# Up and gated projections with stationary weights and [high|low] activations as one moving operand

## Chip, cores and metric

One core of one Trainium2 chip. The metric is the device time of one execution in microseconds, the median of several runs. All arithmetic is float32; the matrix products are made exact enough by splitting each operand into a high part (rounded to float32r, "fp32r" in the rows) and a low part (what is left), with three products: high x high, high x low, low x high.

## What is computed

Two transformer blocks on 256 tokens of width 1024. Cut to what the change touches:

```python
# first block
h2 = rmsnorm(x, g_norm2) * (1.0 + scale2) + shift2
x = x + gate2 * (jnp.square(jax.nn.relu(h2 @ w_mlp1)) @ w_mlp2)      # 1024 -> 4096 -> 1024

# second block: four times (two layers, two each)
def swiglu(x, w_gu, w_down):                                           # 1024 -> 2 x 2816 -> 1024
    g, u = jnp.split(x @ w_gu, 2, axis=-1)
    return (jax.nn.silu(g) * u) @ w_down
x = layer_norm(DEEPNORM_ALPHA * x + 0.5 * swiglu(x, w_gu[i, j], w_down[i, j]), ln_g, ln_b)
```

Around these stand two attentions with their projections and a pooling mixer, which the change leaves alone.

## The kernel before

**Weight units.** All large weights come as units of 2 MB, listed by `weight_units` (L72). A wide unit is 1024 input rows by 512 output columns (8 k-tiles of 128 x 512); a deep unit is 512 rows by 1024 columns. The units of this case are `("up", 0..7)`, each with 512 hidden features, and `("gu", f, 0..10)` for the four gated layers f (f0 to f3 below), each with 256 columns of g and 256 of u, then the `down` and `dn` units behind them. A gated layer runs gu 0 to 6, dn 0 to 3, gu 7 to 10, dn 4 and 5. `up` runs 0 to 3, down 0 to 3, up 4 to 7, down 4 to 7.

**Each unit is used for two blocks**, token half 0 and token half 1. `PAIRS` (L124) names units which go with their neighbour as (u,0), (u+1,0), (u,1), (u+1,1): up 0 and 1, gu 0 and 1, down 6 and 7, dn 4 and 5 are such pairs. All others go (u,0), (u,1).

**Four engines, each with one hand-written order.** SyncE loads a unit in two halves into RAW (`raw_load`, L563), a half when the half before it is split. ScalarE rounds four quarters into WH (`round_unit`, L1176, row line L1187), VectorE subtracts into WL (`split_unit`, L1555, row line L1564). WH and WL hold two units. TensorE multiplies. Each engine works its list strictly in order and waits on semaphores.

**A wide block (L738)** is 8 k-tiles of the helper `three` (L724): three matmuls of 512 moving columns, the weights moving (WH, WL, WH), the activations of 128 tokens stationary (AH, AH, AL). The result, tokens by 512 features, stands in one PSUM bank: UP has two banks, used in turn. `up_phase` on ScalarE (L1416) applies Relu or Silu to it (row line L1429), on VectorE (L1905) a product gives TMP (L1920). The deep products want features on the partitions, so TensorE turns TMP with transposes into a TB bank (`from_tmp`, L799, row line L796; four 128x128 blocks for `up`, two for `gu`), always after the block that follows. ScalarE rounds the turned tile to HH (`high`, L1190, row line L1193), VectorE writes HL (`low`, L1567, row line L1570) and so frees the TB bank, of which there are two.

**In `up_phase` of ScalarE and VectorE** the next unit's rounding and splitting stand ahead of a unit's first block; then the block's own activation and product; then the `late` tile, the one turned since. After the last wide block `down_phase` (L1440, L1932) first rounds and splits the unit behind the first deep one, then handles the late tile.

**Deep blocks (L758, `down_phase` L1035)** read HH and HL of one token half; before each block `ready` waits until `need[i]` of that token half is there.

Of the kernel before, what the change touches and what calls it, by code (L numbers as in the profile page):

```python
# [26 lines left out]
P = 128  # L27
TOK = 2
# [117 lines left out]

def wide_keys(first, end):

    return [UNITS[u][0] + (tok,) for u, tok in WIDES if first <= u < end]


def psum_turns():
# [36 lines left out]
    return {k: i for i, k in enumerate(keys)}  # L189


TURN = psum_turns()
# [4 lines left out]
def counts(chosen):  # L197

    n, out = 0, {}
    for k in TURN:  # L200
        if chosen(k):
            n += 1
            out[k] = n
    return out


SPLIT_NO = counts(lambda k: k[0] not in PLAIN)
TMP_S = counts(lambda k: k[0] in BY_SCALAR)
TMP_V = counts(lambda k: k[0] not in BY_SCALAR and k[0] not in ("col", "h", "tab", "ada", "F", "pool", "y", "my"))
TG_NO = counts(lambda k: k[0] in ("up", "gu"))  # L210
TG_AT = {n: TMP_V[k] for k, n in TG_NO.items()}


def key_kt(key):

    return 4 * (key[1] % 4) if key[0] == "up" else 2 * (key[2] % CUT)

# [16 lines left out]
def build(nc, t, out):  # L234
    with ExitStack() as ctx:
# [13 lines left out]
        AH = sb("AH", [P, KT, 256], F32R)  # L249
        AL = sb("AL", [P, KT, 256], F32R)  # L250
# [79 lines left out]
        UP = [bank(f"UP{i}") for i in range(TOK)]  # L330
        Y = [[bank(f"Y{i}{h}") for h in range(2)] for i in range(TOK)]
        TB = [bank(f"TB{i}") for i in range(2)]
# [23 lines left out]
        tg_done = sem("tg_done")  # L356
        s_done = sem("s_done")
# [61 lines left out]
        up_emptied = []  # L419
        copies = 0  # L420
        for u, tok in WIDES:
            name = UNITS[u][0]
            k = name[0]
            if k == "misc":
                up_emptied.append((lf_in, tok + 1))
            elif k in ("vd", "vf", "gate") or (k == "moba" and name[1] >= 4):
                copies += 1
                up_emptied.append((up_copied, copies))
            elif k in BY_SCALAR:
                up_emptied.append((tmp_s, TMP_S[name + (tok,)]))  # L430
            elif k == "up":
                up_emptied.append((tg_done, TG_NO[name + (tok,)]))
            else:
                up_emptied.append((tmp_v, TMP_V[name + (tok,)]))

        def up_bank(u, tok):

            return Y[1][tok] if u == 1 else UP[WIDE_NO[u, tok] % 2]

# [283 lines left out]
        def _(pe):  # L723
# [14 lines left out]
            def wide(u, tok, chain=None, turns=None, head=None):  # L738

                _, _, width, kts = UNITS[u]  # L740
                pe.wait_ge(*up_emptied[WIDE_NO[u, tok] - (4 if u == 2 else 2)])
                ts = slice(tok * P, (tok + 1) * P)
                dst = up_bank(u, tok)
                for k in range(kts):
# [10 lines left out]
                    quarter_taken(mm, u, tok, (k + 1) * width)  # L755
                mm.then_inc(mm_done, 1)
# [25 lines left out]
            def bank_of(key):  # L782
                b = TURN[key]
                if b >= 2:
                    pe.wait_ge(*emptied(b - 2))
                return TB[b % 2]
# [236 lines left out]
            def up_phase(units, blocks, chain, buf, late):  # L1023

                first = UNIT[units[0]]
                for u, tok in [blk for blk in WIDES if first <= blk[0] < first + len(units)]:
                    opening = chain and u < first + 2
                    wide(u, tok, chain if opening else None,
                         (chain, 1, buf) if opening and (u, tok) == (first + 1, 0) else None)
                    for k in late:  # L1030
                        from_tmp(k, blocks)
                    late = [UNITS[u][0] + (tok,)]
# [135 lines left out]
        def _(act):  # L1168
# [21 lines left out]
            def high(key, dst, n):  # L1190
# [3 lines left out]
                         ).then_inc(th_done, 1)  # L1194

# [219 lines left out]

            def up_phase(units, nblk, func, chain, late):  # L1416
                first = UNIT[units[0]]
                n = P * nblk
                for u, tok in [blk for blk in WIDES if first <= blk[0] < first + len(units)]:
# [6 lines left out]
                    act.wait_ge(mm_done, MM_NO[u, tok])  # L1426
                    if TG_NO[key] > 2:
                        act.wait_ge(tmp_v, TG_AT[TG_NO[key] - 2])
                    act.activation(tg_of(key)[:, 0:n], up_bank(u, tok)[:, 0:n], func).then_inc(tg_done, 1)  # L1429
# [7 lines left out]
                    late = [(key, HH[:, k0:k0 + nblk, tok * P:(tok + 1) * P])]  # L1437
                return late

            def down_phase(units, late, n, last=False):  # L1440
                for i, unit in enumerate(units):
                    if not (last and i == len(units) - 1):
                        round_unit(UNIT[unit] + 1)
                    if i == 0:
                        for k, dst in late:
                            high(k, dst, n)
# [100 lines left out]
        def _(ve):  # L1547
# [356 lines left out]

            def up_phase(units, nblk, square, chain, late):  # L1905
                first = UNIT[units[0]]
                n = P * nblk
                for u, tok in [blk for blk in WIDES if first <= blk[0] < first + len(units)]:
# [6 lines left out]
                    b = TURN[key]  # L1915
                    ve.wait_ge(tg_done, TG_NO[key])
                    ve.wait_ge(tr_done, b - 1)
                    tg = tg_of(key)[:, 0:n]
                    other = tg if square else up_bank(u, tok)[:, n:2 * n]
                    ve.tensor_tensor(TMP[:, b % 2, 0:n], tg, other, ALU.mult).then_inc(tmp_v, 1)  # L1920
                    if opening and (u, tok) == (first, 0):
                        chain_low(chain, 1)
                    for k, hi, lo in late:
                        low(k, lo, hi, n)
                    if opening and (u, tok) == (first, 1):
                        split_unit(u + 2, (2, 3))
                    k0 = key_kt(key)
                    at = (slice(None), slice(k0, k0 + nblk), slice(tok * P, (tok + 1) * P))
                    late = [(key, HH[at], HL[at])]
                return late  # L1930

            def down_phase(units, late, n, pieces=0, last=False):  # L1932
                for i, unit in enumerate(units):
                    if not (last and i == len(units) - 1):
                        split_unit(UNIT[unit] + 1)
                    if i == 0:
                        for k, hi, lo in late:
                            low(k, lo, hi, n)
# [153 lines left out]
```

## Time and profile before

| | us |
|---|---|
| median of 3 runs | 1363.24 (1362.72 to 1363.39) |
| span of the profiled execution, first to last instruction | 1361.6 |
| TensorE busy in it | 1333.7 |
| VectorE busy | 824.2 |
| ScalarE busy | 653.3 |
| mean granted TensorE clock | 0.996 of 2.4 GHz |

The median is 1.6 us above the span; I carry that difference unchanged. In rows of a timeline the first number is the start in us from the span's start, the second the duration in us, then engine, line, operation, output<-inputs, shape and count; a bracket at the end gives the idle time just before and what ended it. A matmul's duration includes its way through the array, so the pace of a stream is read from starts, not from durations. An "x4" row is four instructions merged, its duration that of the four.

### The profile page before, as it was taken

Reading aid. Unit: us, or ns where it says so; the run is one execution under the profiler, and the core shown is the slowest. Engines: PE = TensorE matmul, PEld = TensorE weight load, DVE = VectorE, ACT = ScalarE, POOL = GpSimd, SP = SyncE. Lnnn points to the kernel's source line nnn. Section 1 sums busy time; section 2 is a strip of 40 time slices with the busy share of each in tenths; the row PEclk is TensorE's granted clock in tenths of the full one; section 3 lists DMA queues with packets and bytes.
Section 4 is the critical chain, followed back from the end, with each engine's and each line's share of the span. In section 5 each row is a group of like instructions: output and inputs, shape, how many; then the busy total and the mean of one; then the engine's idle time right before and its main releaser. Section 6 shows DMA issues by size and latency. Waiting matters only on the chain.

```text
span 1361.6 us, 16419 instructions
## 1 busy us (share of the span) xinstructions
PE 1333.7 (98%) x6285; PEld 1100.4 (81%) x6285; DVE 824.2 (61%) x1132; ACT 653.3 (48%) x1046; POOL 80.2 (6%) x114
## 2 busy tenths in 40 slices
PE   7999999999999999999999999999999999999997
PEld 6788878888888888888877888888888888888885
DVE  6787667866566554555547554566554566755454
ACT  4675564553454444444665443445443444544342
POOL 1401100100002000001001000001000010100000
PEclk9999999999999999999999999999999999999998
DMA  9957745557555754647516655647645565665551
GB/s 341 320 199 240 268 160 185 185 213 251 185 186 169 231 187 155 206 165 241 192 63 201 201 186 189 211 156 234 201 168 186 186 211 189 208 194 186 190 181 61
DMA packets 160217, 268.38 MB, mean 197 GB/s; under 512 B 9755, under 2 KB 103052, under 8 KB 160012
## 3 DMA queue, kind: packets, MB, share of 16 engines
q1 hardware_dynamic: 152492, 239.49, 51.8%
q0 software_dynamic: 7648, 27.85, 5.7%
q8 instruction: 50, 0.82, 0.2%
q14 instruction: 27, 0.22, 0.1%
HBM read 266.21 MB, written 1.07 MB: 196 GB/s over the span
## 4 chain that ended last, share of the span: by engine, by line
PE 93%; DVE 3%; DMA 1%; issue 1%; ACT 1%; POOL 1%; SPq 0%; DVEq 0%; ACTq 0%; POOLq 0%
PE UP L725 18%; PE UP L727 18%; PE UP L726 18%; PE Y L725 10%; PE Y L727 10%; PE Y L726 10%; PE TB L796 4%; PE Y L828 1%; PE Y L835 1%; DMA WADA<-in_w_ada 0%; DMA ADA<-in_b_ada 0%; DVE ADA L1685 0%; DVE WL L1564 0%; PE TB L871 0%; PE Y L827 0%
## 5 line engine op out<-in xcount | busy, mean ns | idle before, releaser
L1564 DVE TENSOR_TENSOR WL<-RAW,WH 128x1024 fp32r<-128x1024 f32 (+2 forms) x438 | 503.1, 1194 | 185.6 <-ACT WH L1187 180.1
L1187 ACT CAST WH<-RAW 128x1024 fp32r<-128x1024 f32 (+2 forms) x438 | 425.8, 1032 | 219.1 <-PE Y L727 115.7
L725 PE MATMUL UP<-WH,AH 128*128 128x512 f32 (+1 forms) x1120 | 452.4, 404 | 2.9 <-DVE AL L1720 1.3
L727 PE MATMUL UP<-WH,AL 128*128 128x512 f32 (+1 forms) x1120 | 437.4, 391 | 0.0
L726 PE MATMUL UP<-WL,AH 128*128 128x512 f32 (+1 forms) x1120 | 435.9, 389 | 0.0
L725 PEld LDWEIGHTS UP<-WH,AH 128*128 128x128 f32 x1120 | 211.0, 188 | 45.5 <-issue 2.8
L727 PEld LDWEIGHTS UP<-WH,AL 128*128 128x128 f32 x1120 | 210.7, 188 | 45.5
L726 PEld LDWEIGHTS UP<-WL,AH 128*128 128x128 f32 x1120 | 211.5, 189 | 39.9 <-issue 0.2
L725 PE MATMUL Y<-WH,HH 128*128 128x512 f32 (+1 forms) x496 | 193.9, 391 | 0.0
L727 PE MATMUL Y<-WH,HL 128*128 128x512 f32 (+1 forms) x496 | 191.6, 386 | 0.0
L726 PE MATMUL Y<-WL,HH 128*128 128x512 f32 (+1 forms) x496 | 191.4, 386 | 0.0
L1429 ACT ACTIVATE TG<-UP 128x256 f32<-128x256 f32 (+1 forms) x104 | 43.3, 416 | 280.1 <-PE UP L727 280.0
L1920 DVE TENSOR_TENSOR TMP<-TG,UP 128x256 f32<-128x256 f32 x88 | 36.8, 418 | 176.9 <-ACT TG L1429 176.6
L727 PEld LDWEIGHTS Y<-WH,HL 128*128 128x128 f32 x496 | 93.1, 188 | 19.1
L726 PEld LDWEIGHTS Y<-WL,HH 128*128 128x128 f32 x496 | 93.3, 188 | 18.1
L725 PEld LDWEIGHTS Y<-WH,HH 128*128 128x128 f32 x496 | 93.2, 188 | 18.0
L647 POOL TENSOR_SCALAR VAR<-SQ 128x1 f32<-128x1 f32 x18 | 16.8, 935 | 1014.6 <-ACT PR L1205 1011.3
L725 PE MATMUL Y<-WH,AH 128*128 128x512 f32 x144 | 58.0, 403 | 1.0 <-DVE AL L1570 1.0
L727 PE MATMUL Y<-WH,AL 128*128 128x512 f32 x144 | 56.2, 391 | 0.0
L726 PE MATMUL Y<-WL,AH 128*128 128x512 f32 x144 | 56.1, 390 | 0.0
L1193 ACT CAST HH<-TB 128x256 fp32r<-128x256 f32 (+1 forms) x108 | 43.9, 407 | 17.8 <-PE TB L796 14.9
L1570 DVE TENSOR_TENSOR HL<-TB,HH 128x256 fp32r<-128x256 f32 (+1 forms) x108 | 50.5, 468 | 2.7 <-ACT HH L1193 2.2
(236 smaller groups left out, 920.1 us busy)
## 6 DMA issues: line engine op xcount, KB each, us to landing
RAW<-in_ffn_w_gu SPq DMA_DIRECT2D x176, 512.0 KB, 4.9
RAW<-in_ffn_w_down SPq DMA_DIRECT2D x80, 512.0 KB, 4.1
RAW<-in_w_mlp SPq DMA_DIRECT2D x64, 512.0 KB, 4.3
RAW<-in_w_in SPq DMA_DIRECT2D x34, 512.0 KB, 5.5
PIECE<-in_w_ada POOLq DMA_DIRECT2D x32, 512.0 KB, 6.1
RAW<-in_a_w_in SPq DMA_DIRECT2D x24, 512.0 KB, 4.6
WADA<-in_w_ada SPq DMA_DIRECT2D x14, 512.0 KB, 10.1
RAW<-in_w_out SPq DMA_DIRECT2D x8, 512.0 KB, 3.9
```

The source lines that it names most:

```text
L647: step(gp.tensor_scalar(VAR[:, tok:tok + 1], a, b, eps, ALU.add, ALU.add))
L725: pe.matmul(dst, ah, wh, start=first, stop=False)
L726: pe.matmul(dst, ah, wl, start=False, stop=False)
L727: return pe.matmul(dst, al, wh, start=False, stop=last)
L796: mm = pe.transpose(dst[:, i * P:(i + 1) * P], source[:, i * P:(i + 1) * P], order[:, :])
L828: pe.matmul(dst[:, P:REV], q[:, P:256], k[:, 0:256], start=kind == "m", stop=True).then_inc(s_done, 1)
L1187: act.copy(WH[:, u % 2, q * n:(q + 1) * n], raw_half(u, q // 2)[:, (q % 2) * n:(q % 2 + 1) * n]).then_inc(wh_done, 1)
L1193: act.copy(dst, TB[TURN[key] % 2][:, 0:n].rearrange("p (k n) -> p k n", n=dst.shape[2])).then_inc(th_done, 1)
L1429: act.activation(tg_of(key)[:, 0:n], up_bank(u, tok)[:, 0:n], func).then_inc(tg_done, 1)
L1564: ve.tensor_tensor(WL[:, u % 2, o], raw_half(u, q // 2)[:, (q % 2) * n:(q % 2 + 1) * n], WH[:, u % 2, o].bitcast(F32), ALU.subtract).then_ ...
L1570: ve.tensor_tensor(dst, TB[TURN[key] % 2][:, 0:n].rearrange("p (k n) -> p k n", n=dst.shape[2]), hi.bitcast(F32), ALU.subtract).then_inc(t ...
L1920: ve.tensor_tensor(TMP[:, b % 2, 0:n], tg, other, ALU.mult).then_inc(tmp_v, 1)
```

## The change

All `up` and `gu` units except the pairs (up 0, 1 and gu f 0, 1) are computed "by feature": 6 up units and 9 x 4 = 36 gu units. For these, a 128 x 128 piece of the weights is stationary, and the activations move: AH and AL now lie side by side as `AHL`, 512 columns = [256 tokens high | 256 tokens low]. One matmul of WH against all 512 columns and one of WL against the 256 high columns replace the three; the bank then holds high products in columns 0 to 255 and, in 256 to 511, the two corrections. A unit still has two parts, but a part is two 128-feature blocks (for gu: one of g, one of u) for all 256 tokens, in two PSUM banks at once. Even parts use both UP banks (`UPP`), odd parts both TB banks (`TBB`). The result already has features on partitions, so nothing is turned. ScalarE copies the correction columns to TMP, VectorE adds them to the others into TG, then the activation and product follow from SBUF, the rounding to HH and the subtraction to HL from TMP. Numbers of turns (`TURN`) count only what is still turned, and a bank's previous user is looked up in tables.

```diff
+def by_feature(key):
+
+    return key[0] in ("up", "gu") and key[:-1] not in PAIRS and (key[0],) + key[1:-2] + (key[-2] - 1,) not in PAIRS
...
+def turn_banks_before():
+
+    last, out = [None, None], {}
+    for k in ORDER:
+        if not by_feature(k):
+            out[k] = last[TURN[k] % 2]
+            last[TURN[k] % 2] = k
+        elif FEATURE_NO[k] % 2:
+            out[k] = tuple(last)
+            last = [k, k]
+    return out
...
+def feature_kts(key):
+
+    n = 2 if key[0] == "up" else 1
+    k0 = key_kt(key) + n * key[-1]
+    return slice(k0, k0 + n)
...
+        AHL = sb("AHL", [P, KT, 512], F32R)
+        AH, AL = AHL[:, :, 0:256], AHL[:, :, 256:512]
...
+        def turn_bank_free(key):
+
+            return (fs_done, FEATURE_NO[key] + 1) if by_feature(key) else emptied(TURN[key])
+
+        def hidden_ready(key):
+
+            return (fl_done, FEATURE_NO[key] + 1) if by_feature(key) else emptied(TURN[key])
...
+            def feature(u, part, inner=None):
+
+                _, _, width, kts = UNITS[u]
+                key = UNITS[u][0] + (part,)
+                banks = feature_banks(key)
+                order = [(k, block) for k in range(kts) for block in range(2)]
+                if inner is not None:
+                    order.sort(key=lambda kb: kb[1])
+                for k, block in order:
+                    if k == 0:
+                        if block and inner is not None:
+                            from_tmp(*inner)
+                        if FEATURE_NO[key] % 2:
+                            pe.wait_ge(*turn_bank_free(TURNED_BEFORE[key][block]))
+                        else:
+                            pe.wait_ge(*up_emptied[up_before[u, part][block]])
+                    quarters(u, part, (k + 1) * width)
+                    col = k * width + (2 * P * block + P * part if key[0] == "gu" else P * (2 * part + block))
+                    w = slice(col, col + P)
+                    pe.matmul(banks[:, block, :], WH[:, u % 2, w], AHL[:, k, :], start=k == 0, stop=False)
+                    mm = pe.matmul(banks[:, block, 256:512], WL[:, u % 2, w], AH[:, k, :], start=False,
+                                   stop=k == kts - 1)
+                    if block:
+                        quarter_taken(mm, u, part, (k + 1) * width)
+                mm.then_inc(mm_done, 1)
...
@@ up_phase, TensorE
+                    key = UNITS[u][0] + (tok,)
+                    if by_feature(key):
+                        feature(u, tok, (late[0], blocks) if late else None)
+                        late = []
+                        continue
@@ down_phase, TensorE
-                    ready(need[i] + (tok,))
+                    key = need[i] + (tok,)
+                    if by_feature(key):
+                        key = need[i] + (1,)
+                    pe.wait_ge(*hidden_ready(key))
@@ up_phase, ScalarE (behind round_unit(u + 1), as before)
+                        f = FEATURE_NO[key]
+                        act.wait_ge(mm_done, MM_NO[u, tok])
+                        act.wait_ge(tr_done, turned[f % 2])
+                        if f >= 2:
+                            act.wait_ge(fl_done, f - 1)
+                        act.copy(feature_tmp(key).rearrange("p (b n) -> p b n", b=2),
+                                 feature_banks(key)[:, :, 256:512]).then_inc(fc_done, 1)
+                        for k, dst in late:
+                            hidden_high(k, dst, n)
+                        late = []
+                    if by_feature(key) and key[0] == "gu":
+                        act.wait_ge(fs_done, FEATURE_NO[key] + 1)
+                        act.activation(tg_of(key)[:, 0:n], tg_of(key)[:, 0:n], func).then_inc(tg_done, 1)
@@ up_phase, VectorE (behind split_unit(u + 1), as before)
+                        ve.wait_ge(fc_done, FEATURE_NO[key] + 1)
+                        ve.tensor_tensor(tg.rearrange("p (b n) -> p b n", b=2), banks[:, :, 0:256],
+                                         tmp.rearrange("p (b n) -> p b n", b=2), ALU.add).then_inc(fs_done, 1)
+                        for k, hi, lo in late:
+                            hidden_low(k, lo, hi, n)
+                        if square:
+                            ve.wait_ge(fs_done, FEATURE_NO[key] + 1)
+                            ve.scalar_tensor_tensor(tmp, tg, 0.0, tg, ALU.max, ALU.mult).then_inc(tmp_v, 1)
+                        else:
+                            ve.wait_ge(tg_done, LIT_NO[key])
+                            ve.tensor_tensor(tmp[:, 0:n], tg[:, 0:n], tg[:, n:2 * n], ALU.mult).then_inc(tmp_v, 1)
@@ down_phase, ScalarE and VectorE
-                            high(k, dst, n)
+                            hidden_high(k, dst, n)
...
-                            low(k, lo, hi, n)
+                            hidden_low(k, lo, hi, n)
```

`hidden_high` and `hidden_low` do as `high` and `low` did, for a by-feature part from TMP instead of a TB bank; the last of them signals `fl_done`.

## Rows read from the trace of the kernel before

**Rows 1.** The page: busy time by engine, and the chain's shares by engine.
```profile
PE 1333.7 (98%) x6285; PEld 1100.4 (81%) x6285; DVE 824.2 (61%) x1132; ACT 653.3 (48%) x1046; POOL 80.2 (6%) x114
...
PE 93%; DVE 3%; DMA 1%; issue 1%; ACT 1%; POOL 1%; SPq 0%; DVEq 0%; ACTq 0%; POOLq 0%
```

**Rows 2.** Timeline of PE, 1126 to 1133: 512-column matmuls, then twelve of 256 columns.
```profile
1126.88 0.39 PE L725 MATMUL Y<-WH,AH 128*128 128x512 f32 x1
...
1131.41 0.39 PE L727 MATMUL Y<-WH,AL 128*128 128x512 f32 x1
1131.63 0.28 PE L725 MATMUL Y<-WH,HH 128*128 128x256 f32 x1
...
1132.95 0.28 PE L727 MATMUL Y<-WH,HL 128*128 128x256 f32 x1
```

**Rows 3.** Timeline of PE: transposes between blocks, of up (first two) and of gu.
```profile
268.42 0.60 PE L796 MATMUL TB<-IDENT,TMP 128*128 128x128 f32 x4
274.35 0.60 PE L796 MATMUL TB<-IDENT,TMP 128*128 128x128 f32 x4
...
862.56 0.38 PE L796 MATMUL TB<-IDENT,TMP 128*128 128x128 f32 x2
868.25 0.38 PE L796 MATMUL TB<-IDENT,TMP 128*128 128x128 f32 x2
```

**Rows 4.** Timeline of PE, ACT, DVE, 760 to 764: layer f1, end of block (gu 2, 0).
```profile
761.86 0.38 PE L796 MATMUL TB<-IDENT,TMP 128*128 128x128 f32 x2
...
760.55 2.00 ACT L1187 CAST WH<-RAW 128x1024 fp32r<-128x1024 f32 x2 [1.65 <-DMA RAW<-in_ffn_w_gu]
762.46 0.37 ACT L1429 ACTIVATE TG<-UP 128x256 f32<-128x256 f32 x1
...
763.91 0.41 DVE L1920 TENSOR_TENSOR TMP<-TG,UP 128x256 f32<-128x256 f32 x1
```

**Rows 5.** The same place in f0, f2, f3 (PE, DVE) and in up 2 (DVE).
```profile
459.05 0.38 PE L796 MATMUL TB<-IDENT,TMP 128*128 128x128 f32 x2
...
948.77 0.38 PE L796 MATMUL TB<-IDENT,TMP 128*128 128x128 f32 x2
...
1194.63 0.38 PE L796 MATMUL TB<-IDENT,TMP 128*128 128x128 f32 x2
...
462.85 0.41 DVE L1920 TENSOR_TENSOR TMP<-TG,UP 128x256 f32<-128x256 f32 x1
...
951.45 0.41 DVE L1920 TENSOR_TENSOR TMP<-TG,UP 128x256 f32<-128x256 f32 x1
...
1196.60 0.41 DVE L1920 TENSOR_TENSOR TMP<-TG,UP 128x256 f32<-128x256 f32 x1
...
275.58 0.69 DVE L1920 TENSOR_TENSOR TMP<-TG 128x512 f32<-128x512 f32 x1
```

**Rows 6.** Timeline of ACT, up 2: rounding of a turned tile of 512 columns.
```profile
275.04 0.58 ACT L1193 CAST HH<-TB 128x512 fp32r<-128x512 f32 x1
```

**Rows 7.** Timeline of PE, ACT, DVE, 896 to 904: f1, end of (gu 10, 1).
```profile
896.72 0.38 PE L796 MATMUL TB<-IDENT,TMP 128*128 128x128 f32 x2
...
896.92 0.39 ACT L1429 ACTIVATE TG<-UP 128x256 f32<-128x256 f32 x1 [5.05 <-PE UP L727]
...
897.45 3.90 ACT L1187 CAST WH<-RAW 128x1024 fp32r<-128x1024 f32 x4
...
898.55 4.63 DVE L1564 TENSOR_TENSOR WL<-RAW,WH 128x1024 fp32r<-128x1024 f32 x4 [0.45 <-ACT WH L1187]
903.24 0.42 DVE L1570 TENSOR_TENSOR HL<-TB,HH 128x256 fp32r<-128x256 f32 x1
```

**Rows 8.** Windows around a fall of the clock: busy by engine, PEclk, DMA share, GB/s.
```profile
20.00:23.50 3.50, 2.68 (x21) 2.38 (x19) 2.85 (x8) 1.09 (x2) 0.00 (x0) 0.98 1.05 385
23.50:26.50 3.00, 2.94 (x11) 2.94 (x12) 2.79 (x10) 2.13 (x4) 0.00 (x0) 0.50 1.06 388
26.50:30.00 3.50, 3.50 (x22) 3.19 (x22) 3.43 (x4) 0.85 (x1) 0.00 (x0) 0.96 1.05 387
```

More of the change, by code:

```diff
@@ L204, in counts @@
     return out
-SPLIT_NO = counts(lambda k: k[0] not in PLAIN)
+SPLIT_NO = counts(lambda k: k[0] not in PLAIN and not by_feature(k))
 TMP_S = counts(lambda k: k[0] in BY_SCALAR)
@@ L210 @@
 TG_NO = counts(lambda k: k[0] in ("up", "gu"))
+LIT_NO = counts(lambda k: k[0] == "gu" or k[0] == "up" and not by_feature(k))
 TG_AT = {n: TMP_V[k] for k, n in TG_NO.items()}
@@ L419, in build @@
         up_emptied = []
+        up_before = {}
+        up_last = [0, 0]
         copies = 0
-        for u, tok in WIDES:
+        for n, (u, tok) in enumerate(WIDES):
+            fm = FEATURE_NO.get(UNITS[u][0] + (tok,))
+            if fm is None:
+                up_before[u, tok] = (up_last[n % 2],)
+                up_last[n % 2] = n
+            elif fm % 2 == 0:
+                up_before[u, tok] = tuple(up_last)
+                up_last = [n, n]
             name = UNITS[u][0]
@@ L782, in bank_of @@
             def bank_of(key):
[L783 to L786, printed above, removed]
+                before = TURNED_BEFORE[key]
+                if before is not None:
+                    pe.wait_ge(*turn_bank_free(before))
+                return TB[TURN[key] % 2]
             def turn(key, blocks, source, order=IDENT):
@@ L1031, in up_phase @@
                         from_tmp(k, blocks)
-                    late = [UNITS[u][0] + (tok,)]
+                    late = [key]
                 return late
@@ L1914, in up_phase @@
                     key = UNITS[u][0] + (tok,)
[L1915 to L1922, printed above, removed]
@@ L1923, in up_phase @@
-                    for k, hi, lo in late:
-                        low(k, lo, hi, n)
-                    if opening and (u, tok) == (first, 1):
-                        split_unit(u + 2, (2, 3))
+                    n = P * nblk
+                    tg = tg_of(key)
+                    if by_feature(key):
+                        banks = feature_banks(key)
+                        tmp = feature_tmp(key)
+                        ve.wait_ge(fc_done, FEATURE_NO[key] + 1)
[6 more added lines that the diff above has]
+                            ve.scalar_tensor_tensor(tmp, tg, 0.0, tg, ALU.max, ALU.mult).then_inc(tmp_v, 1)
+                        else:
+                            ve.wait_ge(tg_done, LIT_NO[key])
+                            ve.tensor_tensor(tmp[:, 0:n], tg[:, 0:n], tg[:, n:2 * n], ALU.mult).then_inc(tmp_v, 1)
+                    else:
+                        b = TURN[key]
+                        ve.wait_ge(tg_done, LIT_NO[key])
+                        ve.wait_ge(tr_done, b - 1)
+                        other = tg[:, 0:n] if square else up_bank(u, tok)[:, n:2 * n]
+                        ve.tensor_tensor(TMP[:, b % 2, 0:n], tg[:, 0:n], other, ALU.mult).then_inc(tmp_v, 1)
+                        if opening and (u, tok) == (first, 0):
+                            chain_low(chain, 1)
+                        for k, hi, lo in late:
+                            hidden_low(k, lo, hi, n)
+                        if opening and (u, tok) == (first, 1):
+                            split_unit(u + 2, (2, 3))
```

68 lines of the change are left out of this document (51 added, 17 removed).

## The prediction

> **What bounds the kernel now.** I read the page's busy times and chain first: TensorE is busy 98% of the span and the chain of work that ended last is 93% TensorE [rows 1]. So a microsecond taken out of TensorE's own stream comes off the time, and a microsecond in which TensorE waits is added in full. VectorE at 61% and ScalarE at 48% have room on average, but that is an average. The change gives both new links in chains on which TensorE waits, so I then read the timelines of all three engines at the places where by-feature parts begin and end. The question is not whether the work is less, but which waits lose their cover.
>
> **Part 1: what the stream gains.** In steady state a gu block goes from transposes to transposes in 868.25 - 862.56 = 5.69 us, an up block in 274.35 - 268.42 = 5.93 us [rows 3]. Matmuls of 512 columns start every (1131.41 - 1126.88)/20 = 0.2265 us [rows 2]; 24 of them are 5.44 us. What is left is the price of the turning: 0.26 us for two transposes, 0.49 us for four. By-feature parts replace 36 x 2 = 72 gu blocks and 6 x 2 = 12 up blocks: 72 x 0.26 + 12 x 0.49 = 18.7 + 5.9 = 24.6 us off.
>
> A part now has 16 matmuls of 512 and 16 of 256 columns: 16 x 768 = 12288 columns, just as many as 24 x 512. Only the count grows, from 24 to 32. Matmuls of 256 columns start every (1132.95 - 1131.63)/11 = 0.120 us, each with its own weight load [rows 2]. A part is 16 x (0.2265 + 0.120) = 5.54 us, 0.11 us above the 5.44: 84 x 0.108 = 9.1 us on. Bounds: below, if pace were by columns alone, 0.113 us for 256 and nothing on; above, if the load of the next weights didn't fit under 256 columns, the 0.28 us duration of such a matmul would be its pace, 215 us on. The row has exactly these shapes, in float32r, and shows a load hidden, so I take 9.1. The stream gains 24.6 - 9.1 = 15.5 us.
>
> The Trainium skill (TensorE: Matmul & The Clock Gate, section Back-to-back issue gap) gives N/2.4 + 2.5 ns for an isolated warm matmul. By that the eight extra matmuls of a part would cost 84 x 8 x 2.5 ns = 1.7 us, not 9.1. The row shows 13 ns above the columns at 2.4 GHz for both widths, so the trace does not agree with it and I stay with the row.
>
> **Part 2: ScalarE and VectorE in steady state: nothing.** A gu part adds a copy of 512 columns (as 0.58 us, [rows 6]) and an addition of 512 (as 0.69 us, [rows 5]). Per part of 5.54 us ScalarE then has half of 3.90 for rounding, the copy, Silu 0.39 and a rounding of 0.37; VectorE has half of 4.63, the addition, product 0.42 and low 0.42 [rows 7]: 3.3 and 3.8 us, within 5.54. In order: rounding of the next unit begins some 1.6 us after an odd part ends, splitting ends 7.4 us after it, and the addition of the even part at 8.1; TensorE wants that bank pair back at 11.1. The cover is 3 us. It is used up at two places.
>
> **Part 3: a new wait at the first odd part.** Behind the pairs (gu 0, 1 or up 0, 1) comes part (gu 2, 0), with the transposes of the last old-style tile, (gu 1, 1), in its middle. Part (gu 2, 1) needs both TB banks, also the one of (gu 1, 1). That bank is free only after its `low`. This now stands on ScalarE behind the copy of (gu 2, 0), on VectorE behind the addition of (gu 2, 0), and both stand behind rounding and splitting of gu 3, which wait for its load. Before, TensorE needed that bank a block or more later. In f1 TensorE would reach (gu 2, 1) at 761.86 + 0.11 + 0.26 = 762.23 (longer part, transposes inside). VectorE is through with the split at 763.91 [rows 4]; addition 0.69 (the next starts 0.08 earlier, as in the rows), low 0.42 and 0.05 for the signal make 1.07: 764.98, a wait of 2.75 us. The same sum for the others [rows 5]: f0 462.85 + 1.07 - 459.42 = 4.5; f2 952.52 - 949.14 = 3.4; f3 1197.67 - 1195.00 = 2.7. Counting turns without the by-feature ones, the late tile is in bank 0 in f0 and up, in bank 1 in f1 to f3; there TensorE can do one pair of matmuls, 0.35 us, before it stops: 2.4, 3.0, 2.3. For up: arrival 274.35 + 0.11 + 0.49 = 274.95; done signal 0.16 + 0.06, copy 0.58, addition 0.69, low of 512 columns 0.69 and 0.05: 277.18, a wait of 2.2. Sum 4.5 + 2.4 + 3.0 + 2.3 + 2.2 = 14.4 us on. Floor, if the splits were done in time: the chain alone from the part's end, 1.9 us in a gu layer: 4 x 1.9 - 3 x 0.35 + 2.2 = 8.8 us.
>
> **Part 4: a new wait ahead of dn 5.** A hidden tile now holds 128 features of all tokens, so token half 0 of a deep unit needs both parts of a gu unit. The order is (dn 4,0), (dn 5,0), ..., and (dn 5,0) needs (gu 10, 1), which ended one block earlier. Before it needed only (gu 10, 0). ScalarE and VectorE handle that tile behind rounding and splitting of all of dn 5. Rounding began 0.59 us after the block's end (896.86, 0.06 before the activation's row), now after copy 0.58, addition 0.69, Silu: at 1.65, 1.06 later. The split ended 898.55 + 4.63 = 903.18 [rows 7], now 904.24, low 0.42 and signal: 904.71. TensorE ends (dn 4,0) at 896.70 + 5.44 = 902.14. Wait 2.57 us, in each of four layers: 10.3 us on. From below 0 if the tile's low came ahead of the splits, which the order doesn't do. In the other transitions (gu 6 to dn 0, up 3 to down 0, up 7 to down 4) the last tile is needed three or more blocks later: nothing.
>
> **Part 5: the clock.** At 20 to 23.5 us TensorE did one-column matmuls and waited; then the granted clock was 0.50 (1.2 GHz) for 3 us and back at 2.4 GHz after [rows 8]. That costs about 1.5 us each time. The nine new waits are 2.2 to 4.5 us of nothing. I take one fall, at the 4.5 us wait in f0, 1.5 us; from below 0, above 9 x 1.5 = 13.5.
>
> **The sum.** -24.6 + 9.1 + 14.4 + 10.3 + 1.5 = +10.7 us against a span of 1361.6, so 1372.3, plus the 1.6 us between span and median: 1374.
>
> **Rivals.** (a) Not slower: the two waits are mostly covered. The mechanism is at the entry to (gu 2, 1) and (dn 5, 0): ScalarE and VectorE get to the late tile before TensorE does. Against it: the code puts both behind four rounded and split quarters [rows 4, 7]. For it: the wait in part 3 hangs on when a load lands, ScalarE waiting 1.65 us for it in f1 [rows 4], and could shrink to its 8.8 floor. It decides at waits of 15.5 us in all: below that the kernel is no slower. With both covered the stream's gain stands alone, 1363.2 - 15.5 = 1348; with only the dn 5 wait covered, 1363.2 - 15.5 + 14.4 = 1362. (b) The clock falls in most waits: 1374 + 12 = 1386. For it: the waits are as long as the quiet stretch in rows 8. Against it: TensorE is dense on both sides of each. The Trainium skill (same page, HAM oscillation) has idle gaps bring the clock to half; it is the rule behind this rival, and rows 8 agree with it once. (c) The change doesn't do what it says: a stationary piece of weights and a 512-column [high|low] operand stream slower than the row of 256 columns, because the row's moving operand is another tile. 10 ns per matmul, 84 x 32 of them, would be 27 us: about 1400. Nothing in the rows speaks for it.
>
> **How the numbers follow.** Forecast, both waits within a third of their size and none to three falls: 1366 to 1380, chance 0.60, likeliest 1374. Waits small but not gone (half covered), 1358 to 1366: 0.12. Rival (a) in full, 1345 to 1358: 0.13. Rival (b), 1380 to 1388: 0.11. Rival (c): 0.04. The range of eight in ten is 1358 to 1384. A difference under 0.2%, 2.7 us, is about what a measurement of this kernel can't tell from none: faster (below 1360.5) 0.17, same 0.09, slower (above 1366) 0.74.
>
> **What would show it.** Right: parts without transposes every 5.54 us; one gap of 2 to 4.5 us before the second part of gu 2 (up 2), ended by VectorE's low of a TB bank; one of 2.6 us before the second deep block of dn 4 and 5, ended by a low from TMP; TensorE idle up by some 25 us. Wrong: a part longer than 5.6 us (part 1, rival c), no gap at one of the places (parts 3, 4), gaps in steady state before even parts (part 2), or a PEclk well under 0.99 (rival b).

## The result and the profile after

The changed kernel takes 1391.84 us (median of 4 runs, 1388.28 to 1392.80) against 1363.32 for the kernel before: 1.0203 times, 95% interval 1.0191 to 1.0215. The forecast was 1374 with a range of 1358 to 1384, so the direction held and the time lies outside. The profiled execution was the fastest of the four, 1388.28 us, with a mean granted clock of 0.988 where the three others have 0.984 to 0.986; its span is 1386.5 us, 24.9 above that of before.

The page after: busy times, the chain's shares, and the two rows of matmuls that have new idle time ahead of them. This answers to [rows 1].

```profile
PE 1335.3 (96%) x6765; PEld 1123.9 (81%) x6765; DVE 879.4 (63%) x1216; ACT 699.9 (50%) x1118; POOL 77.3 (6%) x114
...
PE 84%; DVE 7%; DMA 4%; ACT 2%; issue 1%; SPq 0%; POOL 0%; DVEq 0%; ACTq 0%; POOLq 0%
...
L841 PE MATMUL TBB<-AHL,WH 128*128 128x512 f32 x672 | 245.3, 405 | 13.1 <-DVE HL L1700 13.1
...
L789 PE MATMUL Y<-WH,HH 128*128 128x512 f32 (+1 forms) x496 | 193.9, 391 | 9.2 <-DVE HL L2041 9.2
```

TensorE's share of the chain fell from 93% to 84%; VectorE and loads are in it now. Its new idle time stands at two lines (elsewhere it differs from before by about 1 us in all): 13.1 us ahead of the first matmul of odd parts, ended by the low of a turned tile (L1700), and 9.2 us ahead of a deep block, ended by a low from TMP (L2041). The list of waits of PE gives total, number and longest of each:

```profile
PE TBB L841 <- DVE HL L1700: 13.1, 5, 4.7
PE Y L789 <- DVE HL L2041: 9.2, 4, 2.3
```

First place, layer f1, timelines of PE, ACT and DVE after. It answers to [rows 4]: ScalarE waits for the load, VectorE splits, and then the two new links (copy and addition) stand ahead of the low that TensorE waits for.

```profile
765.73 0.38 PE L886 MATMUL TBB<-IDENT,TMP 128*128 128x128 f32 x2
...
769.01 0.28 PE L842 MATMUL TBB<-AHL,WL 128*128 128x256 f32 x1
771.60 0.50 PE L841 MATMUL TBB<-AHL,WH 128*128 128x512 f32 x1 [2.31 <-DVE HL L1700]
...
767.17 2.00 ACT L1285 CAST WH<-RAW 128x1024 fp32r<-128x1024 f32 x2 [1.71 <-DMA RAW<-in_ffn_w_gu]
769.07 0.57 ACT L1551 COPY TMP<-UPP 128x512 f32<-128x512 f32 x1
...
768.25 2.36 DVE L1694 TENSOR_TENSOR WL<-RAW,WH 128x1024 fp32r<-128x1024 f32 x2 [1.34 <-ACT WH L1285]
770.53 0.68 DVE L2059 TENSOR_TENSOR TG<-UPP,TMP 128x512 f32<-128x512 f32 x1
771.13 0.41 DVE L1700 TENSOR_TENSOR HL<-TBB,HH 128x256 fp32r<-128x256 f32 x1
```

Second place, layer f0, PE and DVE ahead of (dn 5, 0); [rows 7] showed the same place in f1. The split of four quarters comes first, then the low, then TensorE.

```profile
602.39 0.39 PE L791 MATMUL Y<-WH,HL 128*128 128x512 f32 x1
605.07 0.50 PE L789 MATMUL Y<-WH,HH 128*128 128x512 f32 x1 [2.29 <-DVE HL L2041]
...
606.24 0.63 PE L790 MATMUL Y<-WL,HH 128*128 128x512 f32 x1
606.66 0.63 PE L791 MATMUL Y<-WH,HL 128*128 128x512 f32 x1
...
600.05 4.63 DVE L1694 TENSOR_TENSOR WL<-RAW,WH 128x1024 fp32r<-128x1024 f32 x4 [0.52 <-ACT WH L1285]
604.60 0.42 DVE L2041 TENSOR_TENSOR HL<-TMP,HH 128x256 fp32r<-128x256 f32 x1
```

The two rows at 606 show what else came with the wait: 512-column matmuls start 0.42 us apart, not 0.227. The windows behind the nine waits give the granted clock (PEclk, third from the end of a row, ahead of DMA share and GB/s):

```profile
277.00:282.00 5.00, 4.84 (x19) 4.18 (x20) 0.70 (x2) 0.00 (x0) 0.00 (x0) 0.66 0.59 224
462.20:467.20 5.00, 5.00 (x19) 4.32 (x20) 0.42 (x1) 0.05 (x1) 0.00 (x0) 0.66 0.71 229
605.00:609.00 4.00, 3.93 (x11) 3.14 (x12) 0.01 (x1) 0.00 (x0) 0.00 (x0) 0.62 0.98 360
771.60:777.00 5.40, 5.40 (x30) 4.70 (x31) 0.42 (x1) 0.06 (x1) 0.00 (x0) 1.00 0.64 197
914.00:918.00 4.00, 4.00 (x20) 3.27 (x19) 0.00 (x0) 0.00 (x0) 0.00 (x0) 1.00 1.05 349
965.30:971.00 5.70, 5.68 (x17) 4.84 (x18) 0.42 (x1) 0.09 (x1) 0.00 (x0) 0.50 0.58 187
1109.00:1113.00 4.00, 4.00 (x18) 3.27 (x19) 0.00 (x0) 0.00 (x0) 0.00 (x0) 1.00 0.99 378
1217.00:1222.00 5.00, 5.00 (x22) 4.32 (x21) 0.00 (x0) 0.00 (x0) 0.00 (x0) 0.67 0.62 205
1359.00:1365.00 6.00, 6.00 (x19) 4.78 (x20) 0.00 (x0) 0.00 (x0) 0.00 (x0) 0.72 0.01 3
```

After six of the nine waits TensorE stood at its lower level, 1.2 GHz, for part of the window, after the longest one (f2) for all of it. After the wait of f1's first place and those of f1 and f2 ahead of dn 5 it stayed at 2.4 GHz. Over the span the mean is 0.988, before 0.996. The time at half clock is thus some (1 - 0.988) x 2 x 1386.5 = 33 us against (1 - 0.996) x 2 x 1361.6 = 11 us, 22 us more, and half of it, 11 us, is lost. The means are rounded to 0.001, which makes this 11 us uncertain by some 1.5.

**A third thing** is slower than the forecast: a part. The copies out of PSUM (ACT, L1551) beat the time of the parts. In f1 two odd parts lie 11.30 us apart, 5.65 a part; in f0, behind a fall of the clock, 11.09, 5.55 a part:

```profile
777.20 0.59 ACT L1551 COPY TMP<-TBB 128x512 f32<-128x512 f32 x1 [5.54 <-PE TBB L842]
...
788.50 0.59 ACT L1551 COPY TMP<-TBB 128x512 f32<-128x512 f32 x1 [2.88 <-PE TBB L842]
```

```profile
469.61 0.59 ACT L1551 COPY TMP<-TBB 128x512 f32<-128x512 f32 x1 [7.36 <-PE TBB L842]
...
480.70 0.59 ACT L1551 COPY TMP<-TBB 128x512 f32<-128x512 f32 x1 [2.67 <-PE TBB L842]
```

Taken from the starts of all matmuls at 2.4 GHz, a pair of 512 and 256 columns takes either 347 ns (30 parts) or 353 ns (54 parts), the same through a whole run of parts.

**The sum for the profiled execution**: transposes -24.6; more matmuls +9.1; the slower pace 54 x 16 x 6.5 ns = +5.6; the nine waits, from start to start less the usual interval (0.12 us behind a matmul of 256 columns, 0.227 behind one of 512), 2.16 + 2.53 + 2.47 + 4.82 + 1.93 at the first place (up, f0 to f3), 13.9, and 4 x 2.45, 9.8, at the second, +23.7; the clock +11. Together +24.8, measured +24.9. The first two terms are those of the prediction, and the clock's is uncertain by some 1.5, so that the agreement is closer than the terms are.

### The profile page after: what moved, and what is told of

It is laid out like the page before. It is cut to its first block, busy times and chain, and to the rows that moved or that the text cites. A ratio compares the mean times of both kernels' runs of the same rounds, so it can differ in the third digit from the quotient of the medians.

```text
span 1386.5 us, 17409 instructions
## 1 busy us (share of the span) xinstructions
PE 1335.3 (96%) x6765; PEld 1123.9 (81%) x6765; DVE 879.4 (63%) x1216; ACT 699.9 (50%) x1118; POOL 77.3 (6%) x114
## 4 chain that ended last, share of the span: by engine, by line
PE 84%; DVE 7%; DMA 4%; ACT 2%; issue 1%; SPq 0%; POOL 0%; DVEq 0%; ACTq 0%; POOLq 0%
PE TBB L841 11%; PE UPP L841 10%; PE Y L789 10%; PE Y L791 9%; PE Y L790 9%; PE UPP L789 6%; PE TBB L842 6%; PE UPP L791 6%; PE UPP L790 6%; PE UPP L842 5%; DVE WL L1694 4%; DMA RAW<-in_ffn_w_gu 3%; PE TBB L886 2%; ACT WH L1285 1%; DVE ADA L1815 1%
## 5 line engine op out<-in xcount | busy, mean ns | idle before, releaser
L841 PE MATMUL TBB<-AHL,WH 128*128 128x512 f32 x672 | 245.3, 405 | 13.1 <-DVE HL L1700 13.1
L841 PE MATMUL UPP<-AHL,WH 128*128 128x512 f32 x672 | 239.3, 398 | 0.0
L842 PE MATMUL TBB<-AHL,WL 128*128 128x256 f32 x672 | 191.8, 285 | 0.0
L842 PE MATMUL UPP<-AHL,WL 128*128 128x256 f32 x672 | 188.5, 281 | 0.0
L789 PE MATMUL UPP<-WH,AHL 128*128 128x512 f32 (+1 forms) x448 | 182.6, 408 | 2.0 <-DVE AHL L1850 0.9
L791 PE MATMUL UPP<-WH,AHL 128*128 128x512 f32 (+1 forms) x448 | 174.5, 389 | 0.0
L790 PE MATMUL UPP<-WL,AHL 128*128 128x512 f32 (+1 forms) x448 | 173.9, 388 | 0.0
L841 PEld LDWEIGHTS TBB<-AHL,WH 128*128 128x128 f32 x672 | 129.7, 193 | 45.9 <-DVE HL L1700 14.7
L841 PEld LDWEIGHTS UPP<-AHL,WH 128*128 128x128 f32 x672 | 126.1, 188 | 29.9 <-issue 0.2
L842 PEld LDWEIGHTS TBB<-AHL,WL 128*128 128x128 f32 x672 | 130.5, 194 | 0.0
L842 PEld LDWEIGHTS UPP<-AHL,WL 128*128 128x128 f32 x672 | 127.0, 189 | 0.4 <-issue 0.2
L1551 ACT COPY TMP<-TBB 128x512 f32<-128x512 f32 x42 | 24.7, 587 | 152.6 <-PE TBB L842 152.6
```

Of the source, the lines that this page charges most:

```text
L789: pe.matmul(dst, ah, wh, start=first, stop=False)
L790: pe.matmul(dst, ah, wl, start=False, stop=False)
L791: return pe.matmul(dst, al, wh, start=False, stop=last)
L841: pe.matmul(banks[:, block, :], WH[:, u % 2, w], AHL[:, k, :], start=k == 0, stop=False)
L842: mm = pe.matmul(banks[:, block, 256:512], WL[:, u % 2, w], AH[:, k, :], start=False, stop=k == kts - 1)
L1551: act.copy(feature_tmp(key).rearrange("p (b n) -> p b n", b=2), feature_banks(key)[:, :, 256:512]).then_inc(fc_done, 1)
```

## The experiments

My theory from here (A): the waits are those at the two named places, and the clock falls because of them; the slower pace is a matter of the stream itself. The rival (B): the clock falls because of the by-feature stream, whatever the waits do. The first four runs tell these apart. All diffs are cut to the lines that matter.

### The waits at the first odd part taken away

```diff
@@ up_phase, ScalarE; VectorE likewise with split_unit and hidden_low
+                    if not opening and tok == 0 and late and by_feature(key) and not by_feature(late[0][0]):
+                        round_unit(u + 1, (0, 1))
+                        for k, dst in late:
+                            hidden_high(k, dst, n)
+                        late = []
+                        round_unit(u + 1, (2, 3))
...
```

> The changed kernel, with the late old-style tile rounded and subtracted between the second and third quarter of the next unit, instead of behind the copy and the addition of the first by-feature part. So the TB bank comes free before TensorE asks for it; the five waits before the first odd part (13.9 us in the profile of the changed kernel) should be gone, the four ahead of dn 5 stay. Theory A: the granted clock falls because of the waits. Five of the seven additional 3.4 us stretches at half clock begin at these five waits, some 8 us more; but by-feature parts ran at 347 instead of 353 ns per pair of matmuls after three of them, 26 parts, and 2.7 us of that is lost again: 1391.8 - 13.9 - 8 + 2.7 = 1372 to 1373. Theory B: the clock falls because of the by-feature stream itself, waits or not: 1391.8 - 13.9 = 1378, and PEclk still falls about seven times.

Measured: 1369.39 us, 1.0048 (1.0033 to 1.0063) times the kernel before. The five waits are gone, the four others are there. The run is 22.4 us below the changed kernel, where the waits alone were 13.9; the clock's mean is 0.993 to 0.994 in the four executions, 0.984 to 0.988 in the changed kernel's. In the profile it fell behind two of the four waits that are left, and nowhere else between the opening and the end:

```profile
598.00:604.00 6.00, 5.66 (x25) 4.70 (x26) 0.28 (x1) 0.00 (x0) 0.00 (x0) 1.00 0.87 315
902.00:909.00 7.00, 6.64 (x22) 5.31 (x23) 0.30 (x1) 0.00 (x0) 0.00 (x0) 0.76 0.79 262
1093.00:1100.00 7.00, 7.00 (x32) 5.76 (x32) 1.40 (x5) 0.08 (x1) 0.00 (x0) 1.00 0.57 218
1340.00:1347.00 7.00, 6.86 (x23) 5.50 (x24) 0.09 (x1) 0.00 (x0) 0.00 (x0) 0.76 0.01 2
```

Which of equal waits of 2.45 us bring it down differs from run to run: in the changed kernel those of f0 and f3, here f1 and f3. That speaks for A, and shows that the length of a wait alone doesn't decide. All 84 parts are at 353 ns, which costs 30 x 16 x 6.5 ns = 3.1 us against the profile of the changed kernel. Time lost to half clock is (1 - mean) x span, so the clock gives back some 0.008 x 1380 = 11 us; 13.9 + 11 - 3.1 = 21.8 of the 22.4 us. The expectation was 3 us too high, since it put 8 us to the clock.

### The waits ahead of dn 5 taken away

```diff
@@ down_phase, ScalarE; VectorE likewise with hidden_low
+                if units[0][0] == "dn" and last:
+                    for k, dst in late:
+                        hidden_high(k, dst, n)
+                    late = []
                 for i, unit in enumerate(units):
                     if not (last and i == len(units) - 1):
                         round_unit(UNIT[unit] + 1)
...
```

> The changed kernel, with the last gu tile's rounding and subtraction ahead of the rounding and splitting of dn 5. The waits ahead of (dn 5, 0), 9.8 us, should be gone: the tile's low is ready some 2.7 us after the part's end, TensorE asks after 5.3. Theory A: with the two falls of the clock at these waits gone too, 1391.8 - 9.8 - 3.4 = 1378.6. Theory B: 1382, with the falls still there.

Measured: 1371.90 us, 1.0062 (1.0047 to 1.0077), 19.9 below the changed kernel, more than either theory gave. The second line of the list of waits is gone, the first reads

```profile
PE TBB L841 <- DVE HL L1704: 11.7, 5, 2.8
```

so the f2 wait of 4.7 us is 2.8 in this run, and the five together are 1.4 us shorter. The clock gives most of the surplus. The executions that were not profiled had a mean of 0.984 to 0.986 in the changed kernel and of 0.992 to 0.994 here: some 0.008 x 1380 = 11 us back, not the 3.4 of the two falls in one profile. With 9.8 and 1.4 us of waits that is 22.2 against 19.9 measured, as close as means rounded to 0.001 allow. A's direction; the size was missed by 6.7 us, since I had priced the falls from one execution.

### Both

> Both reorderings: all nine waits gone. Theory A: 1391.8 - 23.7 - 11 + 2.7 = about 1360, mean clock back at 0.996, by-feature pairs at 353 ns throughout (the stream then gains 24.6 - 9.1 - 8.6 = 7 us on the kernel before: 1356). Theory B: 1368 with the clock at 0.988. If by-feature pairs are all at 347 ns: 1348.

Measured: 1355.71 us (1354.40 to 1356.24), 0.9942 (0.9927 to 0.9957) times the kernel before. With both orders mended the change is a gain of 7.9 us. The clock is at 0.996 to 0.997, as before the change, with the by-feature stream in place: B is out. The page's rows of the by-feature matmuls show no idle time:

```profile
L841 PE MATMUL UPP<-AHL,WH 128*128 128x512 f32 x672 | 240.0, 400 | 0.0
L841 PE MATMUL TBB<-AHL,WH 128*128 128x512 f32 x672 | 238.6, 398 | 0.0
```

71 parts are at 353 ns and 13 at 347. The stream by its terms: -24.6 + 9.1 + 7.4 (71 x 16 x 6.5 ns) = -8.1, measured -7.9. The expectation of 1360 was 4 too high because the falls cost more than I had put to them; 1356, worked out from the stream, was right.

### The waits kept, TensorE kept busy in them

```diff
@@ feature, TensorE
+                if FEATURE_NO[key] % 2 and not by_feature(TURNED_BEFORE[key][0]) and TURNED_BEFORE[key][0][0] in ("up", "gu"):
+                    pe.wait_ge(y_free[0], DEEP["mlp" if key[0] == "up" else f"f{key[1]}"])
+                    constant_products(22 if key[:2] == ("gu", 2) else 12, Y[0][0])
@@ down_phase, TensorE
+                    if key[0] == "gu" and key[2] == 10 and tok == 0:
+                        pe.wait_ge(fs_done, FEATURE_NO[key[:-1] + (0,)] + 1)
+                        constant_products(12, UP[0])
                     pe.wait_ge(*hidden_ready(key))
```

> The changed kernel with its nine waits left as they are, but TensorE does products of constants (384 columns) into a free bank ahead of each: 12, some 2.1 us, and 22 in f2. Their result is not used. Theory A: waits cost their length only, the clock stays at 2.4 GHz: 1391.8 - 11 + 2.7 = about 1383 to 1385, mean clock 0.996. Theory B: no change or, as the products add work, above 1391.

Measured: 1377.97 us, 1.0102 (1.0085 to 1.0119), mean clock 0.995 in the profile and 0.997 in the others. In f0 the products (L970) stand where TensorE had waited, and the same stretch as above now has 30 matmuls in place of 19:

```profile
458.82 2.25 PE L970 MATMUL Y<-CMR,IDR 128*128 128x384 f32 x12
461.18 0.50 PE L844 MATMUL TBB<-AHL,WH 128*128 128x512 f32 x1
...
462.20:467.20 5.00, 5.00 (x30) 4.32 (x29) 0.00 (x0) 0.07 (x1) 0.00 (x0) 1.00 0.55 181
```

TensorE is given work that nobody needs and the kernel is 13.9 us faster. No fall is left behind the opening. The 13.9 us are what the falls cost, less what comes back with them: only 11 parts run at 347 ns here against 30 in the profile of the changed kernel, 2.0 us, so that the falls alone are nearer 16. What is left over "both", 1377.97 - 1355.71 = 22.3 us, should be the length of the nine stretches without useful matmuls, and in this run's trace they add up to 22.3 us. (That -7.9, 22.3 and 13.9 sum to the 28.5 us measured shows nothing by itself: they are differences of neighbouring runs.)

### Half of it

The same edit with 6 products in every place.

> The changed kernel with its nine waits, and 6 products of constants (1.0 us) ahead of each, so that 0.8 to 1.4 us of idle time are left in eight of them and some 2 to 3.7 in f2. If the clock falls only when TensorE is idle for most of such a wait, it stays up but perhaps in f2: 1378 to 1380, as with the waits filled. If any wait of this kernel can bring it down, it stays near 1391.

Measured: 1380.91 us (1376.18 to 1383.02), 1.0124 (1.0103 to 1.0145). The idle time left is 7.1 us in five waits at the first place and 4.9 in four at the second. In the profile the clock stays up behind the four of 1.2 us and behind the three of about that length (0.9 to 1.2) at the first place. Two waits of 1.9 us were left, in f1 and f2; it fell behind the one in f2 and at no other of the nine:

```profile
604.00:612.00 8.00, 7.27 (x32) 6.07 (x33) 2.16 (x8) 0.17 (x1) 0.00 (x0) 1.00 0.68 254
...
962.00:970.00 8.00, 7.89 (x36) 6.75 (x37) 0.62 (x3) 0.93 (x3) 0.00 (x0) 0.79 0.41 132
```

### A short wait of the same kind in the kernel before

```diff
@@ down_phase, TensorE
                     ready(need[i] + (tok,))
+                    if names[i][0][0] == "dn" and i == 1 and last:
+                        ready(need[i] + (1,))
```

> The kernel before the change, where (dn 5, 0) also waits for the low part of (gu 10, 1), as the changed kernel does, though it doesn't read it. It is turned behind (dn 4, 0) and its low ends 1.3 us after that block in the trace of before, so four waits of some 1.3 us: if a wait costs its length and is too short to bring the clock down, 1363.4 + 5.2 = 1368.6, with the clock at 0.996. If even such waits bring it down, some 1.7 us more for each.

Measured: 1368.01 us, 1.0038 (1.0025 to 1.0051), +4.6 us for four waits. Each is 1.0 us in the timeline of PE, 3.9 in all, and in the profile the clock behind all four is untouched; one is shown. (One execution that was not profiled had a mean of 0.994 and took 1370.67 us; where its clock fell is not on record.)

```profile
601.10 0.47 PE L725 MATMUL Y<-WH,HH 128*128 128x512 f32 x1 [0.97 <-issue]
```

```profile
600.00:607.00 7.00, 6.03 (x28) 4.92 (x27) 1.08 (x3) 0.37 (x1) 0.00 (x0) 1.00 0.80 289
```

So the dependence on both parts costs about its length when it is short. Here too the tile stands behind four quarters; the changed kernel's wait is longer, since copy, addition and Silu now stand ahead of those quarters (1.06 us by part 4) and TensorE comes earlier without the transposes. With the tile ahead of the quarters no wait is left, as the run without the dn 5 waits showed.

### The pace: order of widths

What is left open is why a pair of matmuls takes 353 ns. The next four kernels all have both reorderings.

```diff
@@ feature, TensorE
                     pe.matmul(banks[:, block, :], WH[:, u % 2, w], AHL[:, k, :], start=k == 0, stop=False)
-                    mm = pe.matmul(banks[:, block, 256:512], WL[:, u % 2, w], AH[:, k, :], start=False,
-                                   stop=k == kts - 1)
+                    if inner is None and not block:
+                        continue
+                    for b2 in ((0, 1) if inner is None else (block,)):
+                        col2 = k * width + (2 * P * b2 + P * part if key[0] == "gu" else P * (2 * part + b2))
+                        w2 = slice(col2, col2 + P)
+                        mm = pe.matmul(banks[:, b2, 256:512], WL[:, u % 2, w2], AH[:, k, :], start=False,
+                                       stop=k == kts - 1)
```

> The kernel with both reorderings (all waits gone), with the four matmuls of a k-tile in the order 512, 512, 256, 256 columns instead of 512, 256, 512, 256. Same instructions, same banks. Theory A: a pair of matmuls takes 353 ns in most parts, not the 347 of the forecast, because widths alternate; in this order it takes 346.5, and the time falls by 84 x 16 x 6.5 ns = 8.7 us less the parts that are fast already, to about 1348. Theory B: the slower pace comes from the side that moves (activations of 512 columns) or from the engines beside it: no change, 1355.7.

Measured: 1350.20 us (1349.28 to 1351.62), 0.9904 (0.9889 to 0.9919), 5.5 below "both". Four parts in layer f1 take 806.66 - 784.37 = 22.29 us, 5.57 each; in "both" 808.31 - 785.70 = 22.61, 5.65 each. The copies of odd parts, first here and then in "both":

```profile
784.37 0.59 ACT L1562 COPY TMP<-TBB 128x512 f32<-128x512 f32 x1 [2.73 <-PE TBB L847]
...
806.66 0.59 ACT L1562 COPY TMP<-TBB 128x512 f32<-128x512 f32 x1 [2.73 <-PE TBB L847]
```

```profile
785.70 0.59 ACT L1557 COPY TMP<-TBB 128x512 f32<-128x512 f32 x1 [2.89 <-PE TBB L842]
...
808.31 0.59 ACT L1557 COPY TMP<-TBB 128x512 f32<-128x512 f32 x1 [2.88 <-PE TBB L842]
```

It is the fastest of all kernels here. Theory B, that it is the side that moves, is out, since that side is the same in both. A's 8.7 us came only in part: 5.57 us a part is 348 ns a pair, where A had 346.5.

The narrow product first, in all k-tiles but the first:

```diff
@@ feature, TensorE; high and low stand for the two products
+                    if k == 0:
+                        pe.matmul(*high, start=True, stop=False)
+                        mm = pe.matmul(*low, start=False, stop=False)
+                    else:
+                        pe.matmul(*low, start=False, stop=False)
+                        mm = pe.matmul(*high, start=False, stop=k == kts - 1)
```

> The kernel with both reorderings, with the 256-column product ahead of the 512-column one in every k-tile but the first. Widths alternate as before. Theory A (alternating widths make the pace) and theory B both expect no change, 1355.7; a change of more than 3 us would mean that it is which weights are loaded under which width that counts.

Measured: 1352.34 us, 0.9924 (0.9907 to 0.9940), 3.4 below "both", just over the bound that I had set; the two intervals overlap, so that the trace has to carry this. Widths alternate as they did, and in f1 a part is 5.60 us on average against 5.65: odd and even parts differ, one at 5.56 us (347 ns a pair), the next at 5.63 (352), by turns. So alternation is not all of it.

Equal widths in runs of four:

```diff
@@ feature, TensorE
+                    steps = [(b2, lowp) for lowp in (0, 1) for b2 in ((0, 1) if inner is None else (block,))]
+                    if k % 2:
+                        steps = steps[::-1]
```

> The kernel with both reorderings, with the four matmuls of a k-tile in the order 512, 512, 256, 256 for even k and 256, 256, 512, 512 for odd k, so that widths change half as often as in the kernel with 512, 512, 256, 256 throughout (1350.2). If each change of width costs some ns, the pair goes from 349 to about 347.5 and the time to some 1348.5; if only the strict alternation 512, 256, 512, 256 is slow, it stays at 1350.

Measured: 1353.44 us, 0.9925 (0.9909 to 0.9942), a part 5.61 us. Fewer changes of width made a part 0.04 us longer than the order 512, 512, 256, 256 did, so a fixed price for each change is out too. The profiled execution also had more of the lower clock in its opening (its mean is 0.994), which explains a part of its time but not the length of a part in f1.

One width:

```diff
@@ feature, TensorE
-                    mm = pe.matmul(banks[:, block, 256:512], WL[:, u % 2, w], AH[:, k, :], start=False,
+                    mm = pe.matmul(banks[:, block, :], WL[:, u % 2, w], AHL[:, k, :], start=False,
                                    stop=k == kts - 1)
```

> The kernel with both reorderings, with the second product over all 512 columns, so that low x low is added too: 32 matmuls of 512 columns in a part. If moving activations stream as moving weights do, a part is 32 x 0.2274 = 7.28 us against 5.65, 84 x 1.63 = 137 us more: 1492, and the pace within parts reads 227 ns with no second mode. Theory B expects the 512-column matmuls at 230 to 234 ns also here, some 1500.

Measured: 1491.31 us, a single execution. Parts follow each other by 7.25 us in the copies:

```profile
808.56 0.59 ACT L1557 COPY TMP<-UPP 128x512 f32<-128x512 f32 x1 [1.22 <-PE UPP L842]
815.81 0.59 ACT L1557 COPY TMP<-TBB 128x512 f32<-128x512 f32 x1 [5.49 <-PE TBB L842]
```

That is 32 x 0.2266: with one width only, moving activations stream as moving weights do, and all 84 parts keep this pace. Here the slower pace appears only with the two widths, and it depends on their order within the k-tile; what in the chip makes 347 or 353 of it, and why it holds through a run of parts, is not settled.

## Why the prediction missed

**What bounds, and the stream's gain (part 1)**: right that TensorE bounds and that the stream gains. The gain with nothing in its way is measured at 7.9 us for "both", half of the 15.5 forecast, and at 13.2 us with the better order. The part for the transposes, 24.6 us, was not measured by itself; it fits the sums above.

**The pace of a part (part 1)**: the term was 9.1 us and is 14.7 in the profile. I took 0.120 us for 256 columns from twelve matmuls of one width [rows 2] and 0.2265 for 512 from others of one width, and added them. No row showed the two in turns. I held both ends of the bound, from 0 to 215, and then took a value to the nanosecond; the 5.6 us are only 6.5 ns on each of 864 pairs. Rival (c) had a slower stream, with 10 ns per matmul, and it is 3 ns; its reason, that the moving operand is another tile, is not the one, since with one width that operand keeps the pace of the rows.

**Steady state (part 2)**: right. In f1 ScalarE and VectorE show the order that was worked out, and TensorE waits at no even part.

**The two waits (parts 3 and 4)**: right in place and cause, and the second also in size: 10.3 us forecast against 9.8, 2.57 in each layer against 2.45. At the first place 14.4 us against 13.9 is in part luck. The waits of up, f1 and f3 came within 0.4 us, but f0 was forecast at 4.5 and is 2.5, f2 at 3.0 and is 4.8, and the two errors cancel. There I had carried over when the load of gu 3 landed before; in f0 ScalarE waited 1.45 us for it where it had waited 3.41, and in f2, after:

```profile
960.90 1.99 ACT L1285 CAST WH<-RAW 128x1024 fp32r<-128x1024 f32 x2 [4.10 <-DMA RAW<-in_ffn_w_gu]
```

ScalarE waits 4.10 us for it, where it had waited 1.50, and in the run without the dn 5 waits the same TensorE wait is 2.8. When this load landed was not fixed to a microsecond from one run to the next.

**The clock (part 5)**: this is the step that failed most. I took one fall at 1.5 us; the falls cost 11 us in the profiled execution, by its mean clock and windows, and 13.9 or more in the medians, by the kernel that keeps TensorE busy. Of the 14.3 us by which the profiled execution missed 1374, the clock is 9.5 and the pace 5.6, with the waits 1.0 shorter; in the three other executions the clock was lower by another 0.002 to 0.004, which is the rest up to 1391.84. The price of a fall was about right (1.5 us; 11 us over six of them is 1.8), the upper bound of 13.5 nearly so; the choice within the bounds was not. The argument against rival (b) was that TensorE is dense on both sides of each wait. It did not hold: the nine waits, with 1.8 to 4.7 us of idle time, brought a fall in six cases, two thirds. At 0.11 the rival's chance was far too low, and its time of 1386 too, as it left out the pace. Rows 8, from which I had argued, were also misread. The stretch ahead of that fall was not quiet for 3 us; TensorE was idle for 0.88 us, behind matmuls of one column:

```profile
17.30 3.54 PE L877 MATMUL UP<-CMR,IDR 128*128 128x384 f32 x12
20.73 1.95 PE L902 MATMUL Y<-ONES,ADA 128*128 128x1 f32 x16
23.57 0.64 PE L725 MATMUL UP<-WH,AH 128*128 128x332 f32 x1 [0.88 <-DVE AL L1720]
```

So they gave a fair price for a fall, but no evidence either way on idle gaps within a dense stream. The Trainium skill (TensorE: Matmul & The Clock Gate, HAM oscillation) has idle gaps lower the clock; six windows of the trace after agree, 0.62 to 0.72 and once 0.50, and three, at 1.00, do not.

**The range**: it ended at 1384 since I treated the fall as a rival apart from the forecast. It is a consequence of the forecast's own waits, so each wait should have been priced at its length plus the chance of a fall. With the chance and the price as measured afterwards that is 24.7 + 9 x 2/3 x 1.8 = 35.5 us rather than 26.2; it gives 1383, and with the pace 1389.

**Rival (a)**, that TensorE's waits are covered, did not occur, but its mechanism is the cure: ScalarE and VectorE get to the late tile in time when it stands behind two quarters at the first place and ahead of all four at the second. For that case 1348 was forecast and 1355.71 measured; the 7.7 us are the pace, and with the better order it is 1350.20.

## What to carry to other kernels

A new wait of TensorE can cost more than its length. Price it with what the clock does afterwards: here nine waits, 22.3 us in all, brought 13.9 us of slower matmuls with them. When an operand's layout changes, ask for each consumer when the last piece that it now needs is written, and what stands ahead of it in the in-order lists of the other engines; moving two small tiles ahead of quarters of a weight unit turned a loss of 2.0% into a gain of 0.6%, and grouping equal widths into one of 1.0%. A pace taken from a run of one shape is no pace for a mixture of two.

## What the runs showed of the hardware

- In the profiled executions, waits with 0.9 to 1.2 us of idle time between dense matmuls (four in the kernel before with its added wait, seven in the half-filled one) were followed by no fall of TensorE's clock. Of the 20 waits with 1.8 us and more (changed kernel nine, first place mended four, dn 5 mended five, half-filled two) 12 were followed by one and 8 were not, for equal waits in equal layers, and others in the next run; both waits of over 2.6 us were. Keeping TensorE on useless products through a wait kept it at 2.4 GHz at all nine places.
- Matmuls of 512 and 256 columns in turns ran in one of two paces, 347 or 353 ns a pair, constant over runs of 3 to 10 parts (17 to 56 us), while VectorE, ScalarE and the loads came and went beside them. With 512 columns alone there was one pace, 227 ns. In the changed kernel the faster pace followed the falls of the clock in up 2, f0, f2 and f3. In "both" it also came without a fall, in up and in f2, and in the half-filled kernel it did not follow the fall in f2, so a fall is neither needed for it nor enough.
